# Weight loads of 1 MB for two granules in place of 512 KB for one, in a two-block transformer kernel

## What is computed

```python
def hybrid_layer(x, ...):
    proj = rms_norm(x, ln1_w) @ w_in
    ...
    x = x + (g_a * (o_a @ w_pa) + g_b * (o_b @ w_pb)) @ w_o
    h = rms_norm(x, ln2_w)
    return x + jnp.square(jax.nn.relu(h @ w_up)) @ w_down

def second_block(x, ...):
    for i in range(2):
        y = fox_branch(h, ...) if i % 2 == 0 else retention_branch(h, ...)
        h = layer_norm(DEEPNORM_ALPHA * h + y, ln_gain[i], ln_bias[i])
    return h
```

## Time and profile before

| | us |
|---|---|
| median of 3 runs | 2699.04 |
| lowest, highest | 2698.00, 2699.55 |
| the profiled execution | 2698.94 |
| its span, first to last instruction | 2697.3 |

### The profile page before, as it was taken

One profiled execution on the slowest core, in us unless ns is written; L12 is line 12 of the kernel. 1 busy time (PEld: TensorE's weight loads), 2 busy tenths in 40 slices (PEclk: granted clock), 3 DMA queues, 4 the chain that ended last, 5 costly groups with the idle time before them and its releaser, 6 DMA issues.

```text
span 2697.3 us, 35657 instructions
## 1 busy us (share of the span) xinstructions
PE 2677.3 (99%) x13041; PEld 2221.5 (82%) x13041; DVE 1900.2 (70%) x2557; ACT 1289.1 (48%) x1607; POOL 90.3 (3%) x107
## 2 busy tenths in 40 slices
PE   9999999999999999999999999999999999999998
PEld 7888888888888888888888888888888888888886
DVE  5765767665778667586678767876586966678766
ACT  6564646544454444344445455445354444444442
POOL 1000111100000000000000100000000000000000
PEclk9999999999999999999999999999999999999999
DMA  8865555556777666666666565666565655666663
GB/s 244 254 188 148 154 148 145 169 176 189 233 179 211 195 193 193 193 192 197 189 194 191 191 171 178 190 180 204 178 199 171 196 178 189 199 180 191 180 214 121
DMA packets 261726, 504.81 MB, mean 187 GB/s; under 512 B 16472, under 2 KB 25736, under 8 KB 260544
## 3 DMA queue, kind: packets, MB, share of 16 engines
q1 hardware_dynamic: 256848, 486.76, 59.5%
q0 software_dynamic: 4688, 15.90, 2.6%
q10 hardware_dynamic: 32, 0.01, 0.0%
HBM read 498.53 MB, written 4.08 MB: 186 GB/s over the span
## 4 chain that ended last, share of the span: by engine, by line
PE 96%; DVE 1%; ACT 1%; issue 0%; DMA 0%; POOL 0%; SPq 0%; DVEq 0%; ACTq 0%
PE acc L296 53%; PE acc L303 27%; PE acc L1985 2%; PE acc L1983 2%; PE acc L1982 2%; PE acc L1942 1%; PE acc L1944 1%; PE acc L1943 1%; PE acc L2096 1%; PE mx L1748 1%; PE acc L2105 1%; PE mx L511 1%; DVE w_lo L272 0%; ACT w_hi L264 0%; PE mx L519 0%; PE mx L343 0%
## 5 line engine op out<-in xcount | busy, mean ns | idle before, releaser
L272 DVE TENSOR_TENSOR w_lo<-raw,w_hi 128x1024 fp32r<-128x1024 f32 x916 | 1121.5, 1226 | 684.5 <-ACT w_hi L264 675.3
L264 ACT ACTIVATE w_hi<-raw 128x1024 fp32r<-128x1024 f32 x916 | 967.4, 1059 | 1225.5 <-PE acc L303 1069.0
L296 PE MATMUL acc<-w_hi,lt_b_hi 128*128 128x512 f32 x1760 | 685.4, 389 | 0.0
L296 PE MATMUL acc<-w_hi,lt_b_lo 128*128 128x512 f32 x1760 | 684.9, 389 | 0.0
L296 PE MATMUL acc<-w_hi,lt_a_hi 128*128 128x512 f32 x1440 | 563.8, 392 | 0.7 <-DVE lt_b_lo L390 0.7
L296 PE MATMUL acc<-w_hi,lt_a_lo 128*128 128x512 f32 x1440 | 562.2, 390 | 0.0
L303 PE MATMUL acc<-w_lo,lt_b_hi 128*128 128x512 f32 x1760 | 473.3, 391 | 0.0
L303 PE MATMUL acc<-w_lo,lt_a_hi 128*128 128x512 f32 x1440 | 393.4, 395 | 0.0
L296 PEld LDWEIGHTS acc<-w_hi,lt_b_hi 128*128 128x128 f32 x1760 | 330.4, 188 | 68.9
L296 PEld LDWEIGHTS acc<-w_hi,lt_b_lo 128*128 128x128 f32 x1760 | 330.5, 188 | 68.3
L303 PEld LDWEIGHTS acc<-w_lo,lt_b_hi 128*128 128x128 f32 x1760 | 329.1, 188 | 67.3 <-DVE w_lo L272 0.2
(11 more groups left out here) (426 smaller groups left out, 1829.5 us busy)
## 6 DMA issues: line engine op xcount, KB each, us to landing
raw<-in_ret_w_in SPq DMA_DIRECT2D x192, 512.0 KB, 3.9
raw<-in_w_in SPq DMA_DIRECT2D x168, 512.0 KB, 3.8
raw<-in_w_up SPq DMA_DIRECT2D x128, 512.0 KB, 3.7
raw<-in_w_down SPq DMA_DIRECT2D x128, 512.0 KB, 4.7
raw<-in_fox_w_in SPq DMA_DIRECT2D x128, 512.0 KB, 4.5
raw<-in_ret_w_out SPq DMA_DIRECT2D x64, 512.0 KB, 4.5
raw<-in_w_o SPq DMA_DIRECT2D x32, 512.0 KB, 4.8
raw<-in_fox_w_out SPq DMA_DIRECT2D x32, 512.0 KB, 4.5
```

What stands on the lines that cost most here:

```text
L264: nc.scalar.activation(w_hi[:, r % 4], raw[:, slot, 2 * half:2 * half + 2, :], ACT.Copy).then_inc(hi_ready, 1)
L272: nc.vector.tensor_tensor(w_lo[:, r % 4], raw[:, slot, 2 * half:2 * half + 2, :], w_hi[:, r % 4].bitcast(F32), ALU.subtract) \
L296: nc.tensor.matmul(acc[par][t][:, :], lt[p][:, kt, t * P:(t + 1) * P], w_hi[:, r % 4, k, :], start=(kt == 0 and p == 0), stop=False)
```

## The change

`load_job` issues one load per chunk, 1 MB, when the low splits of both granules in its place are done, and the load raises one semaphore, `raw_loaded[2 * q]`. `split_hi` waits for that semaphore for both granules of a chunk. The first job's eight loads stay as they are, each with its own semaphore, and `split_hi` waits for those only in job 0. The last job's split, which is written apart, waits for the chunk's semaphore too. Nothing changes on TensorE, VectorE and GpSimd.

```diff
@@ load_job
             for q in range(chunks):
-                w = src(q).rearrange("(j p) n -> p j n", p=P)
-                m = rows // P // 2
-                for half in range(2):
-
-                    wait(sp, lo_ready, J * GPJ + 2 * q + half + 1 - GPJ)
-                    sp.dma_start(raw[:, q, 2 * half:2 * half + 2, :].rearrange("p a b -> p (a b)").rearrange(
-                        "p (j n) -> p j n", j=m), w[:, half * m:(half + 1) * m, :]) \
-                        .then_inc(raw_loaded[2 * q + half], 16)
+                wait(sp, lo_ready, J * GPJ + 2 * q + 2 - GPJ)
+                sp.dma_start(raw[:, q, :, :].rearrange("p a b -> p (a b)").rearrange("p (j n) -> p j n", j=rows // P),
+                             src(q).rearrange("(j p) n -> p j n", p=P)).then_inc(raw_loaded[2 * q], 16)
@@ split_hi
+            first = isinstance(J, int) and J == 0
             J = lin(J)
             for r in range(r0, r1):
                 slot, half = (r % GPJ) // 2, r % 2
-                wait(act, raw_loaded[r % GPJ], (J + (1 + r // GPJ)) * 16)
+                if first and r < GPJ:
+                    act.wait_ge(raw_loaded[r], 16)
+                else:
+                    wait(act, raw_loaded[2 * slot], (J + (1 + r // GPJ)) * 16)
@@ the last job on ScalarE
-                act.wait_ge(raw_loaded[r], (J_LAST + 1) * 16)
+                act.wait_ge(raw_loaded[r // 2 * 2], (J_LAST + 1) * 16)
```

## The result

| | before | after |
|---|---|---|
| median of 5 runs, us | 2699.55 | 2711.35 |
| lowest, highest | 2698.00, 2702.75 | 2710.95, 2713.10 |
| ratio to before, 95% interval | | 1.0044, 1.0033 to 1.0054 |
| span of the profiled execution | 2697.3 | 2709.8 |

The changed kernel is slower by 11.8 us, 0.44%, where +1.3 us was forecast from the median of 2699.55 (2700.8, range 2698.0 to 2704.0). The spans differ by 12.5 us.

The account below looks back on a forecast made before the run. The prediction took the kernel to be bound by TensorE's matmuls, with weights well ahead. Issues 0, steady stretches 0, 802 us 0 and pair g20, g21 +1.8 us gave 2700.8 us from the median 2699.04, range 2698.0 to 2704.0.

Parts of the forecast that it names:

- The bound: Whole kernel: bound by matmuls, TensorE busy 2677.3 of 2697.3 us, weights well ahead; removing 456 load issues gains 0.
- The steady stretches, 0: Around 1000 us: 1 MB loads, issued later and landing in 7.0 us, still arrive 9.6 us before ScalarE wants them; cost zero.
- The stretch at 802 us, 0: Slow landing at 820.6: ScalarE gets the pair's first half about 2.1 us late, TensorE has 3.7 us to spare; cost zero.
- The pair g20, g21, +1.8: Weight granules 20 and 21, job 2: landing at 74.4 behind GpSimd's bias-table store, g20 stalls TensorE 1.8 us.
- g20's later issue leaves no hole: Step for the pair: the queue was not empty at 44.1, so the pair lands as today's second half, 74.4.
- The second rival: The g20 stall also drops TensorE's clock: 1.8 + 1.9 = 3.7 us, 2702.7 us; chance 0.11.
- the largest stall (4.4): Upper bound for the g20 stall: two granules more of backlog after the bias store, landing at 77.1, stall 4.4 us.
- Bytes and their order are the same: Step on what the change removes: 456 issues go, worth zero for TensorE, with the loads' bytes and order unchanged.
- The third rival: Pair g20, g21 lands at 79, during GpSimd's 1.5 MB load issued at 73.93: stall 6.4 us, 2705.4 us; chance 0.09.
- the second burst: GpSimd's 1.5 MB load issued at 73.93, after the bias-table store; weights behind it were again slow, 4.4 us between g24 and g25.

## Why the prediction was wrong

**The bound.** Right: TensorE has only two new waits, and the matmuls took their rate of before.

**The steady stretches, 0.** Right, shown by the kernel with single loads at the two places. The landing of 1 MB, taken as 7.0 us, was 5.0 to 6.5 in the medians.

**The stretch at 802 us, 0.** Right, and by the mechanism given. ScalarE got its half 3.2 us late (827.66, where its rhythm asked for 824.4), against 2.1 in the prediction, and TensorE did not wait: the low split ended at 829.98, 2.5 us before TensorE came to the granule, against 3.7 in the prediction. The sign that was named, a new wait of TensorE at 800 us, is not there.

**The pair g20, g21, +1.8.** The place and the mechanism are right, the size is not. The wait was 1.8 us with the joint signal alone and 2.4 in the changed kernel, since the pair landed 0.7 us later; over the four profiles in which the pair is also issued late it is 2.4 to 3.3. That "g20's later issue leaves no hole" failed by that much; with own signals g20 came 1.5 us later. More costly was the choice to leave out the clock. The second rival priced the dip at 1.9 us and had only 0.11; the dip stood in all four profiled executions that had this wait with the store as it was: eight products of 3.58 to 3.78 us. (Its price from the rows is 0.8 + 1.0 = 1.8, not 1.9, which changes little.) The argument against it, that a wait of 1.2 us had been passed at full clock, was from a shorter wait elsewhere. With the dip the term is 4.2 us, and 2699.04 + 4.2 = 2703.2 in all, still inside the range. The range's top, 2704.0, has room for the largest stall (4.4) or for the stall with the dip, not for the largest stall with the dip (2705.3). ScalarE's wait for these loads grew from 10.5 to 12.0 us, not to 15.

**What the sum lacked, +6.7.** This is the step that failed: "Bytes and their order are the same", with the cost of the later landings looked for among the weights' own readers alone. The order on SyncE's queue is the same, but GpSimd's transfers are held up by weights in flight (the store's 4.4 us against 2.1), and the change doubles what comes at once ahead of such a transfer. The term that it put at nothing measured 4.6 us of waiting and 2.1 us of slower products. The trace of before had the rows: the store at 1518.78, the load at 1521.20 with a landing of 6.2 us, and VectorE's use at 1527.81, under half a microsecond behind. None of the rivals had a transfer other than weights come late. Had the prediction gone through GpSimd's waits for transfers as it went through ScalarE's, this chain would have been found: it is a wait of 1.9 us for a 16 KB store, followed by a load with a user close behind.

**The third rival**, slower because the pair falls into the second burst, did not come about: the pair landed at 75.1, before 78.1.

**The clock near 200 us, +1.7,** was not in the sum either. The time varies between executions of one kernel: 33 runs of the kernel before spread from 2698.6 to 2703.3, the eleven longest with a mean granted clock of 0.997 and the others with 0.998. In the profiles here the slow products stand at one or both of two places, near 191 to 196 and 214 to 220 us, without a wait ahead of them. The kernel with the doubled store, which is the kernel before up to 1519 us, had both in its profile, so the change is not needed for it; no run shows that it has any share, and this part has a size and no cause.

The Trainium skill's rule ("DMA: Bandwidth & Descriptors", section Bandwidth), that transfers should be batched to 1 MiB, had been weighed as worth nothing here, and that held: 58 jobs with 1 MB loads ran in the same time as with 512 KB.

## What to carry to other kernels

Before grouping transfers, list every transfer of the other queues whose consumer follows within a microsecond of its landing, the small ones first: a larger burst ahead of them delays them (here 2.3 us for the store and 2.6 for the load), and if the consumer is an engine that works in order without idle time, the delay reaches the end nearly whole. A joint signal sets each member's arrival to that of the last, which is free where the cushion is many granules deep and costs in full where a slow transfer beside it has used the cushion up. And when a stall of TensorE is forecast, price the products behind it at the lower clock too: here that doubled a stall of 1.8 us, and it came after all but one of the waits of 1.8 to 3.3 us.

## What the runs showed of the hardware

A 16 KB store of GpSimd took 1.8 to 2.3 us in the five profiles where weights came as single loads of 512 KB, and 4.3 to 4.7 us in the five where 1 MB came at once (2.1 and 4.4 in the two kernels compared, the 1 MB issued 2.9 us ahead of the store). A second store with a load of 512 KB issued 1.1 us ahead of it took 3.5, so the moment counts as well. The 512 KB load after the first store took 6.2 us before and 8.8 after. One transfer of 1 MB and two of 512 KB back to back gave nearly the same figures for it (8.82 and 8.76).

A store that reads 8 partitions and repeats them 128 times to DRAM took 34 us for 1.5 MB, and as long in two parts at once, with nearly double the engine time (77.0% of 16 engines from 40 to 74 us against 43.9%).

After TensorE waits of 1.8 to 3.3 us for one granule, its granted clock was at the lower level for most of what followed (0.50 to 0.58 on average over the 4 or 5 us from 75 or 76 us on), and the next eight products took 3.6 to 3.8 us in place of 1.8. The kernel with the store in halves waited 3.0 us and its next eight products took 2.14, so the dip does not always come whole. After the waits of 3.6 to 4.6 us near 1550 us the three groups of products behind them lost 1.5 to 2.7 us in all.
